# A fused decoder layer on one core: one low part of the seven-product blocks on GpSimd, drains in another order, one barrier between stages, sample taps dealt over tiles, fold turns a stage earlier

## The chip, the cores and the metric

The kernel runs on one core of one Trainium2 chip. The metric is the device time of one execution in microseconds (us), the median of three runs. Its engines are PE (TensorE, matrix products; PEld is its weight load), DVE (VectorE), ACT (ScalarE), POOL (GpSimd) and SP (SyncE, which here starts most transfers). Each has its own instruction list and runs it in order; they meet only at semaphores.

## The reference

One layer over 2048 prompt rows and 8 x 4 sample rows of width 1024, all in float32:

```python
h = rms_norm(x, norm1_g) * (1 + sc1) + sh1          # sc, sh, g from silu(c) @ w_ada + b_ada
q, k, v, u = jnp.split(h @ w_in, ...)               # 512, 512, 512, 1024 columns
q, k = rms_norm(q per head), rms_norm(k per head)
o_attn = attend(q, k, v)                            # three dilated windows, merged
glu = u[..., :512] * sigmoid(u[..., 512:])
dw = causal depthwise conv of width 31 over [history; glu], + bias
o_conv = silu(layer_norm(dw)) @ w_pw2
x = x + g1 * (concat[o_attn, o_conv] @ w_o)
h2 = rms_norm(x, norm2_g) * (1 + sc2) + sh2
x = x + g2 * (square(relu(h2 @ w_ff1)) @ w_ff2)     # 1024 -> 4096 -> 1024
```

The outputs are x for prompt and sample rows, the keys and values of the window, and the last 30 GLU rows.

## The kernel before

Every large product is made of three PE products: each operand is split into a rounded high part (ACT writes it) and a low part, the difference (DVE or POOL writes it), and PE adds high x high, high x low and low x high. The names end in `_hi` and `_lo`.

The program is a row of stages, each one `nc.Block()` with its own instruction lists for the five engines. The times are those of the profile below:

- stage 1, 0 to 65 us: conditioning vectors (`mod`), weights `vu_w`, the first two row tiles. `modulate(i)` (L498) scales tile i into `h_full`, `low_second` (L673) writes the low part of tile 1.
- stage 2 (`vu_`), 66 to 385: values and GLU for 17 row tiles (one has the 32 sample rows). `partial(q)` (L1035) and `select(q)` (L1045) are small PE steps for a quarter of the later conditioning vectors; `products(i, columns)` (L1010) are the large ones.
- stage 3 (`qk_`), 386 to 605: queries and keys for 17 tiles; tile 0 of this stage is the one with the sample rows. PE runs `products(u)`; ACT squares; DVE takes sums, inverse roots (`head_norms`) and the key's gain (`key_gain`). DVE also has the sample rows' convolution here, 31 taps, and 80 late steps of the prompt's (`late_op`, L302).
- stage 4 (`pa_`), 606 to 879: attention of the prompt. Stage 5 (`sa_`), 880 to 959: attention of the sample rows.
- stage 6 (`mx_`), 960 to 1231: layer norm, the products with `w_pw2` and `w_o`, the second norm. It begins with 16 PE turns (transposes) of `w_pw2`, which ACT copies out (L2371), and then folds `w_pw2` into `w_o`, eight groups of products (L2613).
- stage 7 (`ff_`), 1232 to 2624: the MLP, in 3 runs over rows (352, 352 and 336 columns wide per half), each of 8 blocks over the hidden width. In runs 1 and 2, blocks 1 to 6 are "seven-product" blocks: a 2 x 2 product by seven products of sums. Their operands for the second product are 14 high parts on ACT (`sum_high`) and 14 low parts on DVE (`seven_low_part`); the sums they come from are `seven_sum` on DVE. PE's results of the second product leave in 28 drains, `accumulate_seven(b, d)` (L3413), also on DVE. The last two sums (6 and 7) are `zz[0]` and `zz[3]`, the sources of low parts 12 and 13, which both belong to operand S4, the one that PE uses last. POOL writes the low parts of the weights (L3126, 128x512 each, a ring of `WR = 7` slots) in the order in which PE takes them.

Between two stages stands `end_stage()`. The Block itself closes with a barrier of all engines; then:

```python
            nc.clear_and_free_semaphores(list(stage_sems))
            stage_sems.clear()
            nc.all_engine_barrier()
```

The clear runs on POOL, so the stage boundary has two barriers and a clear between them. It is called at six places.

## Time and profile before

| | |
|---|---|
| runs | 2627.72, 2631.33, 2631.54 us; median 2631.33 us |
| profiled execution | 2625.87 us, span of the trace 2624.0 us |
| granted clock of TensorE, mean | 0.986 |
| busy | PE 2521.2 us (96%), DVE 1902.5 (73%), ACT 1282.2 (49%), POOL 1256.0 (48%) |
| instructions | 46483 |

The span runs from the first to the last instruction of the trace; the profiled execution's own time has 1.9 us more around it. The median of the runs is 5.5 us above the profiled execution. PE is busy nearly all the time, so what matters is where it still stands idle, and where it runs at the lower of its two clocks (a granted clock of 0.5 instead of 1).

### The profile page before, as it was taken

How to read it: one execution, taken by the hardware profiler on the slowest of the kernel's cores; microseconds unless marked ns; L12 is line 12 of the kernel's file. 1: busy time of each engine (PE TensorE's matmuls, PEld its weight loads, DVE VectorE, ACT ScalarE, POOL GpSimd, SP SyncE). 2: the span in 40 equal slices, each digit the busy share in tenths (PEclk: the TensorE clock that was granted, in tenths of full speed). 3: DMA queues.
4: the chain of work that ended last, by engine and by line, in shares of the span. 5: the costliest groups of instructions: out<-in, count | busy, mean ns of one | idle time of the engine just before them, and what ended most of it. 6: DMA issues, size and time to landing. Idle time of an engine off the chain costs nothing.

```text
span 2624.0 us, 46483 instructions
## 1 busy us (share of the span) xinstructions
PE 2521.2 (96%) x16058; PEld 2234.5 (85%) x16058; DVE 1902.5 (73%) x4173; ACT 1282.2 (49%) x3188; POOL 1256.0 (48%) x846
## 2 busy tenths in 40 slices
PE   6999989998999889998999999999999999999998
PEld 3788857886777647887999999999999999999998
DVE  4268889997999657876866666566777776667776
ACT  4443313448898534655444333435554453555443
POOL 0000000007999015664655555546676674767673
PEclk9999999998999999999999999999999999999999
DMA  7867625843445884664457766565555566555443
GB/s 298 287 214 238 207 95 188 288 139 119 142 142 164 303 331 149 190 219 128 144 198 256 252 231 226 192 200 167 181 182 181 178 192 214 184 173 158 133 133 125
DMA packets 362198, 507.85 MB, mean 194 GB/s; under 512 B 29338, under 2 KB 277894, under 8 KB 352102
## 3 DMA queue, kind: packets, MB, share of 16 engines
q1 hardware_dynamic: 340090, 455.45, 52.8%
q0 software_dynamic: 4272, 39.19, 4.2%
q10 hardware_dynamic: 17604, 10.24, 1.3%
q8 instruction: 131, 2.15, 0.3%
q14 instruction: 101, 0.83, 0.1%
HBM read 405.10 MB, written 171.81 MB: 220 GB/s over the span
## 4 chain that ended last, share of the span: by engine, by line
PE 22%; POOL 17%; issue 12%; DVE 2%; ACT 0%; POOLq 0%; DMA 0%; SPq 0%; DVEq 0%; ACTq 0%
POOL ff_w_lo L3126 14%; PE ff_u_ps L3646 5%; PE ff_u_ps L3648 5%; PE ff_u_ps L3647 5%; POOL over_acc L3126 2%; PE opening_ps L3646 2%; PE opening_ps L3648 2%; PE opening_ps L3647 2%; PE ff_out_ps L3641 0%; DVE ff_h_hi L3335 0%; DVE ff_h_lo L3338 0%; DVE ff_e L3328 0%; DVE ff_e L3330 0%; POOLq L2793 0%; DVE ff_e L3325 0%
## 5 line engine op out<-in xcount | busy, mean ns | idle before, releaser
L3126 POOL TENSOR_TENSOR ff_w_lo<-gluT,ff_w_hi 128x512 fp32r<-128x512 f32 x450 | 629.1, 1408 | 383.3 <-ACT ff_w_hi L3175 381.2
L3175 ACT ACTIVATE ff_w_hi<-gluT 128x512 fp32r<-128x512 f32 x450 | 278.5, 625 | 295.2 <-PE ff_u_ps L3648 184.2
L3646 PE MATMUL ff_u_ps<-ff_a_hi,ff_w_hi 128*128 128x352 f32 (+1 forms) x696 | 225.1, 323 | 17.6 <-DVE ff_a_lo L3403 14.3
L3648 PE MATMUL ff_u_ps<-ff_a_hi,ff_w_lo 128*128 128x352 f32 (+1 forms) x696 | 223.6, 321 | 0.0
L3647 PE MATMUL ff_u_ps<-ff_a_lo,ff_w_hi 128*128 128x352 f32 (+1 forms) x696 | 223.2, 321 | 0.0
L1780 ACT ACTIVATE pa_score<-pa_score,pa_stat 128x256 f32<-128x256 f32 (+1 forms) x384 | 172.4, 452 | 31.6 <-DVE pa_stat L1722 29.2
L3646 PE MATMUL ff_u_ps<-ff_h_hi,ff_w_hi 128*128 128x352 f32 (+1 forms) x548 | 176.0, 321 | 0.5 <-POOL ff_w_lo L3126 0.5
L3648 PE MATMUL ff_u_ps<-ff_h_hi,ff_w_lo 128*128 128x352 f32 (+1 forms) x548 | 175.4, 320 | 0.0
L3647 PE MATMUL ff_u_ps<-ff_h_lo,ff_w_hi 128*128 128x352 f32 (+1 forms) x548 | 175.0, 319 | 0.0
L302 DVE SCALAR_TENSOR_TENSOR vu_dwp<-gluT,tapT,vu_dwp 128x512 f32<-128x512 f32 x240 | 161.1, 748 | 0.8 <-DVE rstd L210 0.8
L1021 PE MATMUL vu_z_ps<-vu_w_hi,last_hi 128*128 128x512 f32 (+1 forms) x384 | 152.1, 396 | 2.5 <-DVEq L959 2.5
L1022 PE MATMUL vu_z_ps<-vu_w_lo,last_hi 128*128 128x512 f32 (+1 forms) x384 | 150.3, 391 | 0.0
L1023 PE MATMUL vu_z_ps<-vu_w_hi,last_lo 128*128 128x512 f32 (+1 forms) x384 | 150.1, 391 | 0.0
L3646 PEld LDWEIGHTS ff_u_ps<-ff_a_hi,ff_w_hi 128*128 128x128 f32 x696 | 131.6, 189 | 20.7 <-DVE ff_a_lo L3403 16.5
L3647 PEld LDWEIGHTS ff_u_ps<-ff_a_lo,ff_w_hi 128*128 128x128 f32 x696 | 131.9, 189 | 0.0
L3648 PEld LDWEIGHTS ff_u_ps<-ff_a_hi,ff_w_lo 128*128 128x128 f32 x696 | 131.4, 189 | 0.0
L3646 PE MATMUL opening_ps<-ff_a_hi,ff_w_hi 128*128 128x352 f32 (+1 forms) x368 | 119.3, 324 | 8.0 <-DVE ff_a_lo L3403 7.1
L3126 POOL TENSOR_TENSOR over_acc<-gluT,over_dwq 128x512 fp32r<-128x512 f32 x75 | 104.8, 1397 | 40.4 <-ACT over_dwq L3175 40.0
L3648 PE MATMUL opening_ps<-ff_a_hi,ff_w_lo 128*128 128x352 f32 (+1 forms) x368 | 118.6, 322 | 0.0
L3647 PE MATMUL opening_ps<-ff_a_lo,ff_w_hi 128*128 128x352 f32 (+1 forms) x368 | 118.4, 322 | 0.0
L1620 POOL TENSOR_SCALAR pa_tap_x<-gluT,tapT 128x1024 f32<-128x1024 f32 x40 | 113.9, 2847 | 3.0
L2584 PE MATMUL mx_z_ps<-mx_wo_hi,mx_m_hi 128*128 128x512 f32 (+1 forms) x272 | 110.6, 406 | 0.0
(559 smaller groups left out, 7718.7 us busy)
## 6 DMA issues: line engine op xcount, KB each, us to landing
gluT<-in_w_ff_dram SPq DMA_DIRECT2D x196, 256.0 KB, 3.4
gluT<-in_w_ff_dram SPq DMA_DIRECT2D x64, 512.0 KB, 5.3
gluT<-tu_d SPq DMA_DIRECT2D x112, 256.0 KB, 3.0
gluT<-td_d SPq DMA_DIRECT2D x96, 256.0 KB, 3.2
out_new_k_sample_dram<-in_cache_k_dram SPq DMA_DIRECT2D x40, 511.0 KB, 5.2
out_new_v_sample_dram<-in_cache_v_dram SPq DMA_DIRECT2D x40, 511.0 KB, 5.4
dwq<-in_w_ada_dram SPq DMA_DIRECT2D x32, 512.0 KB, 8.6
gluT<-in_cache_k_dram SPq DMA_DIRECT2D x16, 1024.0 KB, 8.8
```

What stands on the lines that cost most here:

```text
L302: return v.scalar_tensor_tensor(out=out, in0=x, scalar=tap(j, c), in1=out, op0=ALU.mult, op1=ALU.add)
L1021: pe.matmul(z, hi, w_hi[:, k, cols], start=k == 0, stop=False)
L1022: pe.matmul(z, hi, w_lo[:, k, cols], start=False, stop=False)
L1023: mm = pe.matmul(z, lo, w_hi[:, k, cols], start=False, stop=k == KT - 1)
L1620: step(pool.tensor_scalar(tap_x[:], gluT[:, c, j + SEQ - LATE:j + SEQ], tap(j, c), None, ALU.mult))
L1780: act.activation(prob[:, u % 4, hh, cols], score[:, u % 4, hh, cols], ACT.Exp, bias=stat[:, p, t, 0, h:h + 1], scale=-1.0, accum_out=stat[ ...
L2584: pe.matmul(z_ps[c][0:n], hi, wo_hi[:, k, cols], start=k == 0, stop=False)
L3126: pool.tensor_tensor(slot_view(w_lo, s), src, slot_view(w_hi, s).bitcast(F32), ALU.subtract).then_inc(w_lod, 1)
L3175: act.activation(slot_view(w_hi, s), src, ACT.Copy).then_inc(w_hid, 1)
L3646: pe.matmul(out, w_hi[s % WR][:, w], hi, start=first, stop=False, skip_group_check=more)
L3647: pe.matmul(out, w_hi[s % WR][:, w], lo, start=False, stop=False, skip_group_check=more)
L3648: return pe.matmul(out, w_lo[s % WR][:, w], hi, start=False, stop=last, skip_group_check=more)
```

## The change

Seven places are edited.

1. `end_stage` only collects the semaphores; a new `clear_ended` clears them on POOL just before the next Block. The second barrier is gone. The next stage uses other semaphores.
2. Stage 1: tile 1 is modulated half by ACT and half by DVE, and split in halves, as tile 0 was.
3. Stage 2: PE's `products(1, (1,))` goes ahead of `partial(0)`, and `select(0)` goes behind `products(1, (2,))`. SP no longer waits at the end of the stage for the store of the window's GLU rows; ACT waits for it in stage 3.
4. Stage 3: PE takes both column halves of tile 0 for each row k of the weights, as their low parts arrive. DVE's 31 sample taps, which stood ahead of the first `head_norms`, are dealt over tiles 1 to 12, two or three to a tile. ACT's load of the Exp table is issued ahead of the last tile's scaling; the last query store no longer waits for the keys.
5. Stage 5 now holds the PE turns of `w_pw2` with their copies, and the turn of the first convolution tile. They write to PSUM buffers that both stages share. On SP the loads of `w_pw2` and `w_o` go ahead of six loads of `mx_stat`.
6. Stage 7, seven-product blocks, DVE: sum 7 goes one drain earlier, low part 12 goes from behind drain 20 to behind drain 17.
7. The same blocks: low part 13 leaves DVE for POOL (`last_low`), ahead of a weight's low part.

The diff, cut to its core:

```diff
 
     whole = ExitStack()
     with whole:
-        stage_sems = []
+        stage_sems, ended_sems = [], []
 
         def sem(name):
             stage_sems.append(nc.alloc_semaphore(name=name))
@@ -126,9 +126,14 @@
 
         def end_stage():
 
-            nc.clear_and_free_semaphores(list(stage_sems))
+            ended_sems.extend(stage_sems)
             stage_sems.clear()
-            nc.all_engine_barrier()
+
+        def clear_ended():
+
+            if ended_sems:
+                nc.clear_and_free_semaphores(list(ended_sems))
+                ended_sems.clear()
 
         def keep(name, shape, dt=F32):
...
@@ -704,7 +704,9 @@
                                 if k == 3:
                                     v.wait_ge(late_in, 32)
                                 table(k)
-                        low_second()
+                        modulate_half(1)
+                        low_half(1, 0)
+                        low_half(1, 1)
 
             end_stage()
...
@@ -1066,12 +1068,12 @@
                         pe.sem_inc(z_pe, NC)
                         products(1, (0,))
                         turn_hist(0)
+                        products(1, (1,))
                         partial(0)
-                        products(1, (1,))
                         turn_hist(1)
-                        select(0)
                         turn_x(2)
                         products(1, (2,))
+                        select(0)
                         partial(1)
                         pe.wait_ge(hist_cp, 2)
                         turn_glu(0)
...
@@ -1360,7 +1372,9 @@
                         v.wait_ge(gain_in, 16 * 3)
                         v.tensor_scalar(qgain[:], qgain[:], -float(DH) ** -0.5, None, ALU.mult).then_inc(gain_set, 1)
                         view = lambda t: t[:].rearrange("p c (b t) -> p c b t", t=DS)
-                        for j in range(TAPS):
+
+                        def sample_tap(j):
+
                             w = tapT[:, j * CC:(j + 1) * CC].unsqueeze(2).unsqueeze(3).to_broadcast([P, CC, DB, DS])
                             if j == 0:
                                 step(v.tensor_tensor(view(dwS), gluS[:, :, :, j:j + DS], w, ALU.mult))
@@ -1368,7 +1382,9 @@
                             else:
                                 step(v.tensor_tensor(view(dwT), gluS[:, :, :, j:j + DS], w, ALU.mult))
                                 step(v.tensor_tensor(dwS[:], dwS[:], dwT[:], ALU.add))
-                        v.sem_inc(dw_done, 1)
+                            if j == TAPS - 1:
+                                v.sem_inc(dw_done, 1)
+
                         for u in range(NT + 1):
                             if u < NT:
                                 head_norms(u)
...
@@ -1379,6 +1395,8 @@
                             for o in range(QK_OPS * u // (NT - 1), QK_OPS * min(u + 1, NT - 1) // (NT - 1)):
                                 late_op(v, cstep, o)
                             key_gain(u)
+                            for j in range(TAPS * max(u - 1, 0) // (NT - 4), min(TAPS * u // (NT - 4), TAPS) if u else 0):
+                                sample_tap(j)
                         cstep.need(cstep.last)
 
                     @block.tensor
...
+
+                        def first_products():
+
+                            n = rows_of(tile_at[0])
+                            for k in range(KT):
+                                pe.wait_ge(w_lod, k + 1)
+                                hi, lo = h_hi[0][:, k, 0:n], h_lo[0][:, k, 0:n]
+                                for c in range(2):
+                                    z, cols = z_ps[c][0:n, :], slice(c * 512, (c + 1) * 512)
+                                    pe.matmul(z, hi, w_hi[:, k, cols], start=k == 0, stop=False)
+                                    pe.matmul(z, hi, w_lo[:, k, cols], start=False, stop=False)
+                                    mm = pe.matmul(z, lo, w_hi[:, k, cols], start=False, stop=k == KT - 1)
+                                    if k == KT - 1:
+                                        mm.then_inc(z_pe, 1)
 
                         def turn_qk(u):
                             n = rows_of(tile_at[u])
...
@@ -1897,6 +1935,9 @@
                     sp.wait_ge(o_done, 1)
                     store_sample(sp, 0)
                     sp.dma_start(mx_dwt[:, 0], dw_d[:, :, 0:P]).then_inc(dw_in[0], 16)
+                    sp.wait_ge(k_pe, 8 * DB)
+                    sp.dma_start(wp_raw, I["w_pw2"][0].rearrange("(k p) c -> p k c", p=P)).then_inc(wp_in, 16)
+                    sp.dma_start(wl_raw, I["w_o"][0, AW:D, :].rearrange("(k p) c -> p k c", p=P)).then_inc(wl_in, 16)
                     sp.wait_ge(pa_st_out, 16 * 3)
                     rows = mx_stat[:].rearrange("p a i s h -> p a i (s h)")
                     sp.dma_start(rows[:, 0], st_d[0]).then_inc(stat_in, 16)
@@ -1904,9 +1945,6 @@
                     for m in range(4):
                         sp.dma_start(rows[:, 1, m:NT:4], by_row[m].rearrange("p (n c) -> p n c", n=NT // 4)).then_inc(stat_in, 16)
                     sp.dma_start(rows[:, 2], st_d[2].rearrange("i r c -> (i r) c").rearrange("(a p) c -> p a c", p=P)).then_inc(stat_in, 16)
-                    sp.wait_ge(k_pe, 8 * DB)
-                    sp.dma_start(wp_raw, I["w_pw2"][0].rearrange("(k p) c -> p k c", p=P)).then_inc(wp_in, 16)
-                    sp.dma_start(wl_raw, I["w_o"][0, AW:D, :].rearrange("(k p) c -> p k c", p=P)).then_inc(wl_in, 16)
                     sp.dma_start(mx_dwt[:, 1], dw_d[:, :, P:2 * P]).then_inc(dw_in[1], 16)
 
...
@@ -2001,6 +2039,17 @@
                             for c in range(4):
                                 turn(AHEAD, c)
                         values(g)
+                    pe.wait_ge(wp_in, 16)
+                    for j in range(CC):
+                        if j == 3:
+                            pe.wait_ge(wt_d, 1)
+                        for k in range(CC):
+                            mm = pe.transpose(fold_ps[j % 3][:, k * P:(k + 1) * P], wp_raw[:, k, j * P:(j + 1) * P], ident[:])
+                        mm.then_inc(wt_pe, 1)
+                        if j == 2:
+                            pe.wait_ge(dw_in[0], 16)
+                            for c in range(CC):
+                                pe.transpose(opening_ps[1][:, c * P:(c + 1) * P], mx_dwt[:, 0, c], ident[:])
 
                 @block.vector
...
@@ -2595,16 +2641,8 @@
                             mm = pe.transpose(h_ps[:, k, 0:n], x1n[0:n, k * P:(k + 1) * P], ident[0:n, 0:n])
                         mm.then_inc(S["h_pe"], 1)
 
-                    turn_dw(0)
-                    pe.wait_ge(wp_in, 16)
-                    for j in range(CC):
-                        if j == 3:
-                            pe.wait_ge(S["wt_d"], 1)
-                        for k in range(CC):
-                            mm = pe.transpose(fold_ps[j % 3][:, k * P:(k + 1) * P], wp_raw[:, k, j * P:(j + 1) * P], ident[:])
-                        mm.then_inc(S["wt_pe"], 1)
+                    pe.sem_inc(S["dw_pe"], 1)
                     pe.wait_ge(wl_in, 16)
-                    pe.wait_ge(S["wt_d"], CC)
                     for g in range(NF):
...
@@ -3141,6 +3181,13 @@
                         pool.wait_ge(sq_d, e + 1)
                         pool.tensor_tensor(a_lo[:, f, tok], z[e % 4][:, 0:w], a_hi[:, f, tok].bitcast(F32), ALU.subtract).then_inc(alo_d, 1)
 
+                    def last_low(b):
+
+                        w = RUNS[b // BLKS][1]
+                        pool.wait_ge(ahi_d, LOW0[b] + 14)
+                        pool.tensor_tensor(operand(a_lo, s_lo, "S4", 1, w), seven_source("S4", 1)[:, 0:w],
+                                           operand(a_hi, s_hi, "S4", 1, w).bitcast(F32), ALU.subtract).then_inc(alo_d, 1)
+
                     pool.sem_inc(w_lod, 1)
                     pool.sem_inc(ahl_p, 4)
...
@@ -3162,6 +3209,8 @@
                         for k in range(DOWN_SLOTS[b]):
                             if blk == BLKS - 1 and run < NR - 1 and k in (1, 3):
                                 h_low(run + 1, k)
+                            if SEVEN[b] and k == 8:
+                                last_low(b)
                             low(SLOT0[b] + up_slots(b) + k + WR)
 
...
@@ -3582,16 +3631,11 @@
                             accumulate_seven(b, 14)
                             seven_sum(b, 6)
                             accumulate_seven(b, 15)
+                            seven_sum(b, 7)
                             accumulate_seven(b, 16)
-                            seven_sum(b, 7)
                             accumulate_seven(b, 17)
-                            accumulate_seven(b, 18)
-                            accumulate_seven(b, 19)
-                            accumulate_seven(b, 20)
                             seven_low_part(b, 12)
-                            accumulate_seven(b, 21)
-                            seven_low_part(b, 13)
-                            for d in range(22, 28):
+                            for d in range(18, 28):
                                 accumulate_seven(b, d)
                             continue
                         for d in range(DN):

```

What DVE does around the sums and low parts of S4, in the first seven-product block. `ff_zz0` and `ff_zz3` are sums 6 and 7 and the sources of low parts 12 and 13; `ff_y` and `ff_e` rows are drains. Before:

```order
L3397 TENSOR_TENSOR ff_zz0_17111<-ff_zz0_17111,gluT 128x352
L3430 TENSOR_TENSOR ff_y<-opening_ps1,ff_y 128x352
L3430 TENSOR_TENSOR ff_y<-ff_u_ps2,ff_y 128x352
L3397 TENSOR_TENSOR ff_zz3_17114<-ff_zz3_17114,ff_z3_13377 128x352
L3430 TENSOR_TENSOR ff_y<-ff_u_ps3,ff_y 128x352
L3430 TENSOR_TENSOR ff_y<-ff_u_ps4,ff_y 128x352
L3430 TENSOR_TENSOR ff_y<-ff_u_ps5,ff_y 128x352
L3428 COPY ff_e167<-opening_ps0 128x352
L3403 TENSOR_TENSOR ff_a_lo<-ff_zz0_17111,ff_a_hi 128x352
L3428 COPY ff_e167<-opening_ps1 128x352
L3403 TENSOR_TENSOR ff_a_lo<-ff_zz3_17114,ff_a_hi 128x352
```

The same place on DVE in the changed kernel:

```order
L3446 TENSOR_TENSOR ff_zz0_17049<-ff_zz0_17049,gluT 128x352
L3479 TENSOR_TENSOR ff_y<-opening_ps1,ff_y 128x352
L3446 TENSOR_TENSOR ff_zz3_17052<-ff_zz3_17052,ff_z3_13357 128x352
L3479 TENSOR_TENSOR ff_y<-ff_u_ps2,ff_y 128x352
L3479 TENSOR_TENSOR ff_y<-ff_u_ps3,ff_y 128x352
L3452 TENSOR_TENSOR ff_a_lo<-ff_zz0_17049,ff_a_hi 128x352
L3479 TENSOR_TENSOR ff_y<-ff_u_ps4,ff_y 128x352
L3479 TENSOR_TENSOR ff_y<-ff_u_ps5,ff_y 128x352
L3477 COPY ff_e167<-opening_ps0 128x352
L3477 COPY ff_e167<-opening_ps1 128x352
```

The second sum moved up by one drain, the first low part by three, and the second low part is gone from this engine. It stands on POOL now, among the weights' low parts of the same block:

```order
L3166 TENSOR_TENSOR ff_w_lo3<-gluT,ff_w_hi3 128x512
L3166 TENSOR_TENSOR ff_w_lo4<-gluT,ff_w_hi4 128x512
L3188 TENSOR_TENSOR ff_a_lo<-ff_zz3_17052,ff_a_hi 128x352
L3166 TENSOR_TENSOR ff_w_lo5<-gluT,ff_w_hi5 128x512
L3166 TENSOR_TENSOR ff_w_lo6<-gluT,ff_w_hi6 128x512
```

Before, the same four weight rows followed one another there with nothing between them.

The third place is SP at the end of stage 5, behind the stores of the sample rows' attention. `gluT` is the buffer that holds `w_pw2` and `w_o`. Before:

```order
L1899 DMA mx_dwt<-dw_d 128x4x128
L1902 DMA mx_stat<-st_d 128x256
L1905 DMA mx_stat<-st_d 128x4x16 x4
L1906 DMA mx_stat<-st_d 128x16x16
L1908 DMA gluT<-in_w_pw2_dram 128x4x512
L1909 DMA gluT<-in_w_o_dram 128x4x1024
L1910 DMA mx_dwt<-dw_d 128x4x128
```

In the changed kernel:

```order
L1937 DMA mx_dwt<-dw_d 128x4x128
L1939 DMA gluT<-in_w_pw2_dram 128x4x512
L1940 DMA gluT<-in_w_o_dram 128x4x1024
L1943 DMA mx_stat<-st_d 128x256
L1946 DMA mx_stat<-st_d 128x4x16 x4
L1947 DMA mx_stat<-st_d 128x16x16
L1948 DMA mx_dwt<-dw_d 128x4x128
```

The two weight loads moved past the six loads of `mx_stat`.

## Rows read from the trace of the kernel before

**Rows 1.** The page's first part: busy time of each engine.
```profile
PE 2521.2 (96%) x16058; PEld 2234.5 (85%) x16058; DVE 1902.5 (73%) x4173; ACT 1282.2 (49%) x3188; POOL 1256.0 (48%) x846
```

**Rows 2.** What PE waited for: us in total, times, longest us.
```profile
PE ff_u_ps L3646 <- DVE ff_a_lo L3403: 14.3, 8, 1.9
...
PE qk_z_ps L1399 <- DVE qk_w_lo L1359: 8.3, 3, 5.8
PE opening_ps L3646 <- DVE ff_a_lo L3403: 7.1, 4, 1.9
...
PE vu_q_ps L1042 <- DMA dwq<-in_w_ada_dram: 2.5, 2, 1.6
```

**Rows 3.** PE in a seven-product block of run 1: start, duration, instruction, [idle].
```profile
1933.61 0.43 PE L3646 MATMUL opening_ps<-ff_a_hi,ff_w_hi 128*128 128x352 f32 x1 [1.66 <-DVE ff_a_lo L3403]
1933.88 0.32 PE L3647 MATMUL opening_ps<-ff_a_lo,ff_w_hi 128*128 128x352 f32 x1
```

**Rows 4.** DVE at the same place.
```profile
1928.72 0.51 DVE L3397 TENSOR_TENSOR ff_zz<-ff_zz,ff_z 128x352 f32<-128x352 f32 x1
...
1930.88 1.17 DVE L3403 TENSOR_TENSOR ff_a_lo<-ff_zz,ff_a_hi 128x352 fp32r<-128x352 f32 x1
...
1932.41 1.15 DVE L3403 TENSOR_TENSOR ff_a_lo<-ff_zz,ff_a_hi 128x352 fp32r<-128x352 f32 x1
```

**Rows 5.** ACT and POOL at the same place.
```profile
1929.27 0.50 ACT L3227 ACTIVATE ff_a_hi<-ff_zz 128x352 fp32r<-128x352 f32 x1 [0.28 <-DVE ff_zz L3397]
...
1929.07 2.59 POOL L3126 TENSOR_TENSOR ff_w_lo<-gluT,ff_w_hi 128x512 fp32r<-128x512 f32 x2 [2.39 <-ACT ff_w_hi L3175]
...
1936.54 1.29 POOL L3126 TENSOR_TENSOR ff_w_lo<-gluT,ff_w_hi 128x512 fp32r<-128x512 f32 x1 [1.84 <-ACT ff_w_hi L3175]
```

**Rows 6.** PE at the same wait in three consecutive blocks of run 2.
```profile
2332.26 0.64 PE L3646 MATMUL opening_ps<-ff_a_hi,ff_w_hi 128*128 128x336 f32 x1 [1.93 <-DVE ff_a_lo L3403]
...
2387.68 0.42 PE L3646 MATMUL ff_u_ps<-ff_a_hi,ff_w_hi 128*128 128x336 f32 x1 [1.92 <-DVE ff_a_lo L3403]
...
2441.53 0.65 PE L3646 MATMUL ff_u_ps<-ff_a_hi,ff_w_hi 128*128 128x336 f32 x1 [1.90 <-DVE ff_a_lo L3403]
```

**Rows 7.** POOL's low parts of activations: ns min/median/max, first and last start.
```profile
L3142 POOL TENSOR_TENSOR ff_a_lo<-gluT,ff_a_hi x18: 900/1048/1247, 1250.5 to 2200.3; 128x352 fp32r<-128x352 f32 x12, 128x336 fp32r<-128x336 f32 x6
```

**Rows 8.** `end_stage`'s first and last step, six times: ns, first and last start us.
```profile
L129 POOLq DRAIN  x6: 89/101/129, 65.1 to 1231.2; - x6
...
L131 SPq EVENT_SEMAPHORE  x6: 17/17/17, 65.8 to 1231.9; - x6
```

**Rows 9.** The end of stage 1, in order of time.
```profile
59.65 2.90 ACT L505 ACTIVATE c_all<-mod_both,modT,gain 128x128 f32<-128x128 f32 x8 [3.54 <-PE mod_both L592]
...
63.67 1.22 DVE L675 TENSOR_TENSOR last_lo<-c_all,last_hi 128x1024 fp32r<-128x1024 f32 x1 [2.62 <-ACT last_hi L516]
```

**Rows 10.** SP's wait for the store of the window's GLU rows, end of stage 2.
```profile
SPq L812 <- DMA out_new_conv_sample_dram<-vu_glu: 2.2, 1, 2.2
```

**Rows 11.** DVE lines of stage 3: ns min/median/max, first and last start; a tap's share.
```profile
L1359 DVE TENSOR_TENSOR qk_w_lo<-dwq,qk_w_hi x8: 1220/1225/1226, 387.0 to 398.5; 128x1024 fp32r<-128x1024 f32 x8
...
L1320 DVE TENSOR_REDUCE qk_ssq<-qk_sqr x16: 1199/1214/1220, 420.1 to 585.8; 128x16 f32<-128x1024 f32 x15, 32x16 f32<-32x1024 f32 x1
...
L1369 DVE TENSOR_TENSOR qk_dwT<-gluS,tapT 128x128 f32<-128x128 f32 x30 | 8.8, 294 | 1.0
```

**Rows 12.** Busy time of each engine in the bulk of stage 3, with instruction counts.
```profile
420.00:600.00 180.00, 175.22 (x838) 145.50 (x836) 166.51 (x334) 91.21 (x358) 1.00 (x2) 1.00 0.65 216
```

**Rows 13.** The end of stage 3, ACT.
```profile
602.01 1.28 ACT L1310 ACT_TABLE_LOAD   x1
```

**Rows 14.** SP before the end of stage 5, and PE at the start of stage 6.
```profile
943.21 8.01 SPq L1905 DMA_DIRECT2D mx_stat<-st_d  x4
...
959.61 0.63 PE L2549 MATMUL opening_ps<-ident,mx_dwt 128*128 128x128 f32 x4 [2.80 <-PEq L131]
...
964.81 1.55 PE L2613 MATMUL opening_ps<-gluT 128*128 128x512 f32 x3 [1.19 <-DMA gluT<-in_w_o_dram]
```

99 lines of the change are left out of this document (56 added, 43 removed).

## The prediction

> **What bounds the kernel now.** I read the page's first part first: PE is busy 2521 of 2624 us and no other engine above 1902 [rows 1]. So a change gains only where PE stands idle, or where it runs at its lower clock, and the list of what PE waited for is the next view. Its largest line, in two parts because two PSUM buffers alternate, is the wait of L3646 for a low part from DVE, 21.4 us in 12 waits [rows 2]: one for each seven-product block (6 in run 1, 6 in run 2). It is the only wait in the MLP that repeats. The other lines that the change touches are the wait for the weights' low parts at the start of stage 3 (8.3) and for a conditioning weight in stage 2 (2.5) [rows 2]. What no wait line shows as one sum are the six stage ends, where every engine stands still.
>
> **Seven-product blocks.** PE begins S4 at 1933.61 after 1.66 idle [rows 3]; without the wait it would have begun 1.66 + 0.16 earlier (the interval of two matmuls, where the record of the one before ends 0.16 after the next could start), at 1931.79. Its first matmul then takes 0.43 instead of 0.32 [rows 3], and the next starts 0.27 later instead of 0.16. A block so loses 1.66 + 0.16 + 0.11, about 1.9, in run 1. In run 2 the idle is 1.90 to 1.93 [rows 6], so about 2.15. I take 1.85 and 2.15: 6 x 1.85 + 6 x 2.15 = **24.0 us** if the wait goes wholly.
>
> Does it go? DVE is behind there: it works without a gap, and low part 13 runs 1932.41 to 1933.56, low part 12 1930.88 to 1932.05 [rows 4]. After the change, sum 7 moves ahead of one drain of about 0.43 and so ends near 1928.8 instead of 1929.23 [rows 4]. ACT's rounding of it, 0.50 long, began at 1929.27 right behind the sum [rows 5]; it can begin near 1929.0, since a weight's rounding stands ahead of it, and ends at 1929.5. POOL has nothing to do before 1929.07, for it waits 2.39 for ACT [rows 5], and low part 13 stands ahead of that next weight part. Its price on POOL is not in these blocks of the trace; the nearest rows are POOL's own low parts of the same shape, 0.90 to 1.25, middle 1.05 [rows 7]. I take 1.2, since DVE works on its low part at the same time: 1929.5 to 1930.7. On DVE, low part 12 comes after drain 17, three drains (1.3) earlier: 1929.6 to 1930.8. Both lie 1.0 before PE needs them at 1931.79. So the whole 24.0 is mine, with 1.0 to spare. Lower bound: if low part 13 took 2.5 on POOL and the others slid too, half of the wait would stay.
>
> What POOL does is now later. Its two weight parts start after 1930.7 instead of 1929.07, and it runs up to about 3 us behind with the wait of PE gone. It was idle again ahead of 1936.54, for 1.84 [rows 5], and it has the ring of seven slots, 1.9 us of PE each, ahead. It catches up within the ring. DVE's drains now come one low part (1.15) and one order earlier, so PSUM banks come free earlier. Cost 0.
>
> The GPSIMD Engine Reference page of the Trainium skill (Key points) says that GpSimd shares its SBUF interfaces with VectorE, with contention for DVE instructions that have two SBUF inputs; that speaks against putting the two low parts side by side. In the trace DVE's two low parts take 1.15 and 1.17 with POOL at work on a weight beside them [rows 4, 5], so the rule, where it bites, is already in that duration. If both low parts were stretched by half again, S4 would be ready near 1931.4, still in time, and the sum would not change.
>
> **The clock.** Two of the six waits of run 2 are followed by a first matmul of 0.64 and 0.65 instead of 0.42 [rows 6]: a stretch at the lower of the two clock levels, 1.2 GHz. From 2332.26 to 2387.68, behind such a start, a block takes 55.42; from 2387.68 to 2441.53, behind a start of 0.42, it takes 53.85 [rows 6]. So a slow start costs 1.5. Two of them: **3.0 us**, if the clock stays up when PE doesn't stand idle.
>
> **Six stage ends.** From the drain on POOL to the release of SP the second barrier and the clear take 0.7, at the first (65.1 to 65.8) and at the last (1231.2 to 1231.9) [rows 8]. The clear stays, on POOL alone, beside the next stage's first work. 6 x 0.65 = **3.9 us**.
>
> **Stage 1.** The last chain is 8 ACT steps of 2.90, ACT's rounding, DVE's low part of 1.22 that ends at 64.89 [rows 9]. With four steps on each engine (ACT 1.45), halves of the rounding and of the low part, both engines overlapped, I have the end at 63.8, where PE also ends: **1.1**.
>
> **Stage 2.** PE waits 2.5 for conditioning weights in `partial(0)` [rows 2]. With 24 matmuls of 0.23 (5.5 us) ahead of it, they are there: +2.5. `select` now stands right ahead of `partial(1)`, and the copy between them costs some 0.7 of it. **1.8**. SP's wait at the end of the stage, 2.2 for a store [rows 10], goes; DVE and the other stores end 1.5 to 2 after PE anyway, so I take 0.5 of it.
>
> **Stage 3, a loss.** DVE is as full as PE here: 166.5 and 175.2 busy of 180 [rows 12], and DVE's short instructions leave about 0.04 between one and the next, so it is in truth never idle. `head_norms` begins at 420.1 and again, 15 tiles later, at 585.8 [rows 11]: 11.05 each, the first about 8.4. Before it, from 399.7 (the last low part is 1.22 long from 398.5 [rows 11]), lie the 31 taps, 61 instructions of 0.294 and 0.03 between [rows 11], about 20 us. PE has tiles 0 to 2 ready by then. With the taps dealt, DVE wants tile 0's sums at 399.7, and PE and ACT give them near 402.5: 2.8 idle. Tile 0 takes 8.4, to 410.9; tile 1 is complete near 413.3 (48 matmuls behind tile 0, and its squares; a matmul of 512 columns at 0.23, an estimate from the 0.16 of 352 columns): 2.4 idle. Then two to three taps (1.3 to 1.9) make a tile 13.2 against PE's 12.0 (180 us by 838 matmuls, 56 a tile [rows 12]), so DVE is the later one from there, and it does the same work as before with 5.2 idle put in. The two idles stand at the end of the stage: **-5.1**. PE's own earlier start on tile 0 (some 3 of the 8.3 [rows 2]) isn't cashed, since DVE ends the stage.
> The end of the stage: the table load of 1.28 stood between two of ACT's last copies [rows 13]; it moves to where ACT waits for DVE. With the small activation and the order of stores: **+1.1**.
>
> **Stage 5 to 6.** PE starts at 959.61 and its first fold product at 964.81 [rows 14]: 5.2 of turns and a wait for `w_o`. The turns go ahead of the barrier, behind the last attention products (some 4 us of PE, for which DVE's last steps of 1.8 give cover). The loads go up past `mx_stat`'s, of which the four of L1905 alone hold SP for 8.0 from 943.21 [rows 14], so `w_o` lands some 15 us earlier. The six loads themselves then end later, and the last engine at the barrier is SP or ACT's copy. I take the stage end 2 later and the folds 3.4 earlier after the barrier (PE's 2.80 idle at the start [rows 14] stays). DVE's layer norm loses 1.4 to nobody's wait. **+1.4** beside the 0.65 counted; bounds -3 (SP's loads end late) and +3.
>
> **Sum.** 24.0 + 3.0 + 3.9 + 1.1 + 1.8 + 0.5 - 5.1 + 1.1 + 1.4 = 31.7. The profiled execution took 2625.9, so 2594.2; the median of the runs is 5.5 above it, so **2599.6**. A measurement of this kernel tells about 0.2% (5.3 us) from no change.
>
> **Rivals.**
> - *Stage 3 loses nothing.* PE, not DVE, ends it, so that the idles of DVE are slack and PE's earlier start counts for 3. For it: PE is the busier of the two [rows 12]. Against: DVE's row starts are even to the end. 5 to 8 less: about 2593. Chance 0.15.
> - *Stage 5 grows.* SP's six loads, each behind 3 to 8 us of a full queue [rows 14], end after the turns, and stage 6's norm starts late. 5 more: about 2605. Chance 0.13.
> - *The S4 wait stays in part.* ACT's rounding of sum 7 comes as late as now (1929.27) and POOL takes 2 or more; then S4 is ready at 1932 to 1933, and half of the 27 stays: 2599.6 + 13 = about 2612. Chance 0.10.
> - *Slower.* `last_low` holds POOL's list until ACT has rounded sum 7. Should POOL reach it much earlier than ACT is ready and the weights' low parts behind it come late, PE would wait for them in each of 12 blocks. To eat 31.7 it needs 2.6 a block beyond the ring's cover, that is POOL ending its backlog some 8 us later than I have it; it gives 2637 at 3.1 a block. POOL's idle times of 2.39 and 1.84 speak against it [rows 5]. Chance 0.02.
> - *The wait only moves*: DVE is late elsewhere in the block, at a drain that frees a PSUM bank, and the 27 us stay: near 2627. Chance 0.02.
>
> The forecast itself has 0.58. Its own range is 2595 to 2604; the rivals beside it widen this to 2591 to 2611, which leaves out about 2 in 10. Faster by over 0.2%: 0.58 + 0.15 + 0.13 + 0.10 = 0.96; same 0.02; slower 0.02.
>
> **What would show each step.** The line "PE L3646 <- DVE a_lo" is gone from PE's waits or has turned into one of under 0.3 for POOL; seven-product blocks stand 53.85 apart in both parities of run 2, and under 54 in run 1. All six stage ends have one barrier. `head_norms` starts near 402.5 in stage 3 on this clock, with two DVE idles of 2 to 3, and the stage is 3 to 5 longer. The first fold product comes within 3 us of stage 6's start. I am wrong if S4 is ready later than PE by more than 0.3, if the lower clock comes elsewhere in the MLP, or if DVE's idle in stage 3 isn't given back at its end.

## The result

The changed kernel took 2605.66 us (median of four runs, 2604.75 to 2608.82), the kernel before 2629.52 (2627.44 to 2631.54) beside it: a ratio of 0.9908, 95% interval 0.9894 to 0.9922. That is 23.9 us less, where 31.7 were forecast, 6.1 us above the forecast of 2599.6: outside the prediction's own range of 2595 to 2604, inside the wider one of 2591 to 2611 that takes in the rivals. The profiled execution took 2605.45 us with a span of 2603.3, against 2625.87 and 2624.0 before: 20.4 to 20.7 less. The 3.4 between 20.4 and 23.9 comes from the profiled execution of before, which lay 3.65 below its own median, where that of the changed kernel lay 0.2 below.

The part that was to carry the gain did. From the list of PE's waits in the changed kernel (us in total, times, longest):

```profile
PE qk_t_ps L1447 <- DVE qk_nrm L1367: 7.5, 4, 5.1
...
PE opening_ps L1973 <- DMA gluT<-in_cache_k_dram: 5.9, 1, 5.9
...
PE vu_xt_ps L1009 <- ACT vu_x_nrm L851: 5.1, 1, 5.1
...
PE opening_ps L2651 <- PEq L1899: 3.4, 1, 3.4
```

The 21.4 us of [rows 2] for DVE's low part have no line here at all. But four waits stand at the top that before did not have or had shorter. The seven-product block that answers to [rows 3 to 5], PE first, then DVE, POOL (start, duration, instruction, [idle]):

```profile
1933.37 0.32 PE L3692 MATMUL ff_u_ps<-ff_s_hi,ff_w_lo 128*128 128x352 f32 x1
1933.53 0.32 PE L3690 MATMUL opening_ps<-ff_a_hi,ff_w_hi 128*128 128x352 f32 x1
1933.69 0.32 PE L3691 MATMUL opening_ps<-ff_a_lo,ff_w_hi 128*128 128x352 f32 x1
```
```profile
1931.30 1.20 DVE L3452 TENSOR_TENSOR ff_a_lo<-ff_zz,ff_a_hi 128x352 fp32r<-128x352 f32 x1
```
```profile
1931.16 0.95 POOL L3188 TENSOR_TENSOR ff_a_lo<-ff_zz,ff_a_hi 128x352 fp32r<-128x352 f32 x1 [2.76 <-ACT ff_a_hi L3276]
1932.08 2.84 POOL L3166 TENSOR_TENSOR ff_w_lo<-gluT,ff_w_hi 128x512 fp32r<-128x512 f32 x2
```

PE goes from one operand to the next at its usual 0.16. POOL's low part is done at 1932.1 and DVE's at 1932.5, 1.0 ahead of the matmul at 1933.53: the margin that the prediction had. POOL's took 0.95 where I took 1.2. They don't really run side by side: DVE's began 0.14 behind POOL's and ended 0.38 behind its end. That is the rule in this trace. Of the changed kernel's low parts on DVE (L3452, 128x352 and 128x336), the 36 that began with POOL idle took 0.49 to 0.53 us. Of the 120 that began with POOL at work, 118 ended 0.36 to 0.39 us behind the end of POOL's instruction, however long that made them; the other two began in its last 0.04 and ended that far behind the next one. The same block shows all of it (DVE, then POOL):

```profile
1922.40 0.51 DVE L3452 TENSOR_TENSOR ff_s_lo<-gluT,ff_s_hi 128x352 fp32r<-128x352 f32 x1
1923.27 1.18 DVE L3452 TENSOR_TENSOR ff_s_lo<-gluT,ff_s_hi 128x352 fp32r<-128x352 f32 x1
```
```profile
1922.74 1.33 POOL L3166 TENSOR_TENSOR ff_w_lo<-gluT,ff_w_hi 128x512 fp32r<-128x512 f32 x1 [2.38 <-ACT ff_w_hi L3224]
```

Where did the rest go? I cut each execution at the first PE row of a stage. Each stretch holds the stage and the boundary behind it:

| stretch | before | changed | difference | forecast |
|---|---|---|---|---|
| to stage 2's first product | 66.23 | 64.63 | -1.6 | -1.75 |
| stage 2 | 322.09 | 326.26 | +4.2 | -2.95 |
| stage 3 | 217.80 | 220.82 | +3.0 | +3.35 |
| stage 4 | 274.36 | 272.92 | -1.4 | -0.65 |
| stages 5 and 6 | 354.18 | 354.41 | +0.2 | -2.7 |
| MLP, to its last turn | 1381.56 | 1356.92 | -24.6 | -27 |

Stages 1, 3 and 4 are within 0.8 of the forecast. Stage 2 is 7 us worse than forecast, stages 5 and 6 are 3 worse, the MLP 2.4. One execution of each kernel stands behind the table; a second one of before's code in stages 1 to 6 (the first experiment) had 67.6 and 323.7 in the first two stretches, and was within 0.5 in the others. Stage 2 is the question. Its wait of 5.06 is a new one; the rows around it, of the changed kernel (ACT, SP, POOL):

```profile
102.83 1.06 ACT L834 ACTIVATE vu_x_nrm<-vu_x_in 128x1024 f32<-128x1024 f32 x1 [12.52 <-DMA vu_x_in<-in_x_prompt_dram]
```
```profile
86.57 0.30 SPq L786 DMA_DIRECT2D mod_d<-vu_g_rows  x1
86.91 0.36 SPq L757 DMA_DIRECT2D vu_x_in<-in_x_prompt_dram  x1
```
```profile
85.86 0.52 POOL L174 DMA_DIRECT2D out_new_k_sample_dram<-in_cache_k_dram  x1 [25.61 <-PE vu_z_ps L1025]
```

ACT stands 12.5 us for a row tile that SP asked for at 86.91, right behind its store of `select(0)`'s rows at 86.57. A microsecond ahead of it POOL had asked for a 4 MB copy of cached keys. The list of transfers in that stretch (issues, KB each, us to landing), first of the changed kernel, then of before:

```profile
out_new_k_sample_dram<-in_cache_k_dram POOLq DMA_DIRECT2D x1, 4088.0 KB, 16.0
...
vu_x_in<-in_x_prompt_dram SPq DMA_DIRECT2D x1, 512.0 KB, 15.8
```
```profile
out_new_k_sample_dram<-in_cache_k_dram POOLq DMA_DIRECT2D x1, 4088.0 KB, 18.1
...
vu_x_in<-in_x_prompt_dram SPq DMA_DIRECT2D x1, 512.0 KB, 4.3
```

Before, the load was issued at 90.32 and the copy at 90.98, and the load landed in 4.3. The two issues have changed places, a microsecond apart, and the load lands 11.5 us later; whether the one causes the other is tested below. TensorE's granted clock over the 30 us from 86 was 0.92 in the changed kernel and 1.00 before.

### The profile page after: what moved, and what is told of

Same layout as the page of the kernel before. It is cut to its first block and busy times, and to the rows that moved or that the text cites. A ratio compares the mean times of both kernels' runs of the same rounds, so it can differ in the third digit from the quotient of the medians.

```text
span 2603.3 us, 46434 instructions
## 1 busy us (share of the span) xinstructions
PE 2517.2 (97%) x16058; PEld 2232.5 (86%) x16058; DVE 1893.4 (73%) x4166; ACT 1281.3 (49%) x3185; POOL 1262.4 (48%) x858
```

## The experiments

Each ran beside the kernel before, on the same chip. The chips differ from one series to the next; before's median was 2629.2 to 2630.4 in all of them. Where a text calls a run "the changed kernel", its median is 2605.66 and comes from a series of its own. The runs of one kernel lie up to 6 us apart, so a difference of two medians under some 3 us says little by itself.

**The seven-product edits alone.** The kernel before with parts 6 and 7 of the change, nothing else:

```diff
+                            if SEVEN[b] and k == 8:
+                                last_low(b)
...
                             accumulate_seven(b, 15)
+                            seven_sum(b, 7)
                             accumulate_seven(b, 16)
-                            seven_sum(b, 7)
                             accumulate_seven(b, 17)
-                            accumulate_seven(b, 18)
-                            accumulate_seven(b, 19)
-                            accumulate_seven(b, 20)
                             seven_low_part(b, 12)
-                            accumulate_seven(b, 21)
-                            seven_low_part(b, 13)
-                            for d in range(22, 28):
+                            for d in range(18, 28):
```

> The kernel before with the edits of the seven-product blocks alone (parts 6 and 7 of the change). Theory: these edits carry the whole gain in the MLP. In the changed kernel the stretch from the first to the last seven-product block was 25.8 us shorter (10.8 in run 1, 15.0 in run 2), so here too: span 2624.0 - 26 = 2598, median 26 below the kernel before, which is 2 below the whole change. Rival: part of the MLP's gain comes from the other edits, which moved the stage's start against its transfers; then the gain here is under 20.

2600.44 us; ratio 0.9888 (0.9873 to 0.9903), 29.9 less than before. The MLP stretch was 1357.4, as in the changed kernel. So these edits carry the whole gain, and the other five parts together made the kernel slower: by 5.2 in the medians, by 2.0 in the spans of the profiled executions (2601.3 and 2603.3). The medians give more than the 24.1 of the MLP stretch; stage 1 alone differs by 2 to 3 us from execution to execution (see the last section), so I read sizes from the stretches.

**Order without POOL.** The changed kernel, low part 13 on DVE behind drain 18:

```diff
-                            if SEVEN[b] and k == 8:
-                                last_low(b)
...
                             seven_low_part(b, 12)
-                            for d in range(18, 28):
+                            accumulate_seven(b, 18)
+                            seven_low_part(b, 13)
+                            for d in range(19, 28):
```

> The changed kernel, but low part 13 stays on DVE, one drain behind low part 12; nothing extra on POOL. Theory: by the trace of before, DVE would have low part 12 until 1930.8, a drain of 0.43, and low part 13 until 1932.4, against PE's need at 1931.79: a wait of 0.6 and 0.3 for the slow first matmul, 0.9 in 12 blocks: 11 us slower than the changed kernel. Rival: the order alone is enough, since the order of the drains brought everything forward: within 2 us of the changed kernel, and the S4 wait does not come back.

2612.44 us; 0.9931 (0.9914 to 0.9947), 6.8 more than the changed kernel; MLP 1363.9, 7.0 more. The wait is back, shorter:

```profile
PE ff_u_ps L3690 <- DVE ff_a_lo L3450: 4.2, 8, 0.7
...
PE opening_ps L3690 <- DVE ff_a_lo L3450: 2.1, 4, 0.7
```

6.3 us in 12 waits, where I had 0.6 each. The order alone gives about 17.6 of the 24.6, and with it in place POOL gives the other 7.

**POOL without the order.** The changed kernel, with DVE's sum 7 and low part 12 in their old places:

```diff
                             accumulate_seven(b, 15)
-                            seven_sum(b, 7)
                             accumulate_seven(b, 16)
+                            seven_sum(b, 7)
                             accumulate_seven(b, 17)
+                            accumulate_seven(b, 18)
+                            accumulate_seven(b, 19)
+                            accumulate_seven(b, 20)
                             seven_low_part(b, 12)
-                            for d in range(18, 28):
+                            accumulate_seven(b, 21)
+                            for d in range(22, 28):
```

> The changed kernel with low part 13 on POOL, but DVE's sum 7 and low part 12 back in their old places (behind drains 16 and 20). Theory: low part 12 ends at 1932.05 as before, 0.26 after PE's need of 1931.79, and costs 0.26 + 0.3 a block: 6 to 7 us slower than the changed kernel, the wait line names DVE L3452 with about 0.3 each. Rival: POOL alone does it, no line in the waits and within 2 us.

2615.17 us; 0.9942 (0.9927 to 0.9957), 9.5 more; MLP 1365.8, 8.9 more. PE waits 7.6 us for L3452 in 12 waits, 0.51 each in run 1 and 0.76 in run 2, where I had 0.26. The rows of DVE and POOL say why:

```profile
1935.56 1.55 DVE L3452 TENSOR_TENSOR ff_a_lo<-ff_zz,ff_a_hi 128x352 fp32r<-128x352 f32 x1
```
```profile
1935.44 2.83 POOL L3166 TENSOR_TENSOR ff_w_lo<-gluT,ff_w_hi 128x512 fp32r<-128x512 f32 x2
```

Low part 12 took 1.55 here, in all six blocks of run 1, instead of 1.17 [rows 4]. It began 0.12 behind the start of POOL's first weight part and ended 0.38 behind its end (1936.73). In the kernel before it began 0.51 into one, and so had less of it to stand out: the low part's length is what is left of POOL's instruction, and 0.38. Neither half of the change is enough; each leaves 6 to 8 us of waits. POOL alone gives 15.7 of the 24.6, and with it in place the order the other 8.9.

**`select(0)` back in its place.** The changed kernel, one line moved:

```diff
                         turn_hist(1)
+                        select(0)
                         turn_x(2)
                         products(1, (2,))
-                        select(0)
                         partial(1)
```

> The changed kernel with select(0) of stage 2 back in its place ahead of turn_x(2); products(1, (1,)) stays ahead of partial(0). Theory: in the changed kernel SP stood at the store of select(0)'s result until 86.57 and so issued the load of the next row tile at 86.91, behind POOL's 4 MB-class cache copy of 85.86; the load landed near 102.8 and PE waited 5.06 at 112.86. With select(0) early, SP issues that load ahead of the copy: PE's wait at 112.86 is gone, ACT's wait for the load falls from 12.5 to under 1, at a price of about 0.4 for PE's wait on ACT's copy before select(0): 4 to 5 us less than the changed kernel. Rival: the copy simply comes earlier against the loads, whatever SP does: the wait stays at 4 to 5 us, and the time is that of the changed kernel.

2597.63 us; 0.9876 (0.9862 to 0.9891), 8.0 less than the changed kernel. Stage 2 took 318.1 instead of 326.3. SP and POOL:

```profile
83.03 0.63 SPq L786 DMA_DIRECT2D mod_d<-vu_g_rows  x1
88.47 0.36 SPq L757 DMA_DIRECT2D vu_x_in<-in_x_prompt_dram  x1
```
```profile
89.17 0.53 POOL L174 DMA_DIRECT2D out_new_k_sample_dram<-in_cache_k_dram  x1 [27.52 <-PE vu_z_ps L1025]
```

The load is ahead of the copy again, and PE's wait is gone. The gain is 3 above what I expected, since the clock too stays at 1.00 over the 30 us from 86, and a wait of 0.51 at 86.60 goes.

**The copy later.** `select(0)` stays where the change put it; POOL's first cache copy waits for one more row tile:

```diff
                         for i in (2, 5, 8):
-                            pool.wait_ge(z_pe, NC * i)
+                            pool.wait_ge(z_pe, NC * max(i, 3))
```

> The changed kernel, select(0) where the change put it, but GpSimd's first copy of cached keys in stage 2 waits for one row tile of products more (three instead of two, some 11 us later). Theory: the 5 us wait at 112.86 comes from that copy, issued at 85.86, standing in front of the load of the next row tile, issued at 86.91; with the copy behind the load the wait is gone and TensorE's clock stays up: 7 to 8 us less than the changed kernel, stage 2 at 318 to 319 us as in e4_select_back. Rival: select(0)'s place delays something else (DVE's second mod rows waited 9.2 us for SP's store), the load is late by its own queue: the wait stays above 3 and the time is within 2 us of the changed kernel.

2598.87 us; 0.9886 (0.9869 to 0.9902), 6.8 less than the changed kernel; stage 2 took 318.8, and the load, issued at the same point, is there in time:

```profile
86.19 0.36 SPq L757 DMA_DIRECT2D vu_x_in<-in_x_prompt_dram  x1
```
```profile
90.49 1.06 ACT L834 ACTIVATE vu_x_nrm<-vu_x_in 128x1024 f32<-128x1024 f32 x1 [0.90 <-DMA vu_x_in<-in_x_prompt_dram]
```

So it was the copy in front of the load: with `select(0)` still late and SP still behind its store, moving the copy alone cures it. Stage 2 was 326.3 to 327.3 in all seven kernels that had both, and 318.0 to 318.8 in the four that had the one or the other cured.

**PE's whole order of stage 2 as before.**

```diff
                         turn_hist(0)
-                        products(1, (1,))
                         partial(0)
+                        products(1, (1,))
                         turn_hist(1)
+                        select(0)
                         turn_x(2)
                         products(1, (2,))
-                        select(0)
```

> The changed kernel with PE's whole order in stage 2 as before: partial(0) ahead of products(1, (1,)), select(0) ahead of turn_x(2). Beside e4_select_back it tells what the products ahead of partial(0) are worth. Theory: the 2.5 us waits of partial(0) for the conditioning weights come back, and e4's gain of 3 over the kernel before in this stage goes with them; x_in is loaded in time as in e4: 5 to 6 less than the changed kernel, 2.5 slower than e4_select_back. Rival: GpSimd's copy comes earlier by the one barrier that is gone and still passes the load: the wait of 5 stays and it is slower than the changed kernel.

2603.16 us; 0.9896 (0.9881 to 0.9910), 2.5 less than the changed kernel, 5.5 more than with `select(0)` alone put back. Stage 2: 323.5 against 318.1. The wait that the products had covered is back, and the clock falls behind it:

```profile
74.23 1.08 PE L1044 MATMUL vu_q_ps<-dwq,vu_cT 128*32 128x256 f32 x8 [3.09 <-DMA dwq<-in_w_ada_dram]
...
78.20 0.63 PE L1023 MATMUL vu_z_ps<-vu_w_hi,last_hi 128*128 128x512 f32 x1
```

A product of 512 columns takes 0.63 there instead of 0.39. The products ahead of `partial(0)` are worth 5.4, twice what I took from the wait alone. The waits of `partial(0)` come to 3.5 in this run (3.09 and 0.43) against 2.5 in the kernel before.

**Taps back in front.** The changed kernel, the 31 taps ahead of the loop as before:

```diff
+                        for j in range(TAPS):
+                            sample_tap(j)
                         for u in range(NT + 1):
...
-                            for j in range(TAPS * max(u - 1, 0) // (NT - 4), min(TAPS * u // (NT - 4), TAPS) if u else 0):
-                                sample_tap(j)
```

> The changed kernel with the 31 sample taps back ahead of the first head_norms in stage 3; PE's first_products, the early table load and the last query store stay. Theory: DVE's two idles of 2.39 and 2.42 at tiles 0 and 1 are gone, and since DVE sets the stage's end, stage 3 ends 4.8 earlier: 4 to 5 us less than the changed kernel, and PE's wait of 5.1 for DVE qk_nrm near the end is gone. Rival: PE is the bound and the dealt taps cost nothing: the same time as the changed kernel, within 1 us in stage 3.

2601.01 us; 0.9888 (0.9872 to 0.9904), 4.6 less than the changed kernel; stage 3 took 216.7 instead of 220.8. PE's wait of 5.1 for DVE near the stage's end is gone (one of 5.2 stands at its first turn, where tile 0's norms come after the taps). DVE in the changed kernel, its first two tiles:

```profile
404.44 1.21 DVE L1332 TENSOR_REDUCE qk_ssq<-qk_sqr 32x16 f32<-32x1024 f32 x1 [2.39 <-ACT qk_sqr L1285]
...
415.35 1.22 DVE L1332 TENSOR_REDUCE qk_ssq<-qk_sqr 128x16 f32<-128x1024 f32 x1 [2.42 <-ACT qk_sqr L1285]
```

Two idles of 2.4 at the start of the stage, given back by 4.1 of its end. DVE is the bound, as argued. PE's earlier products of tile 0 and the early table load, which this run keeps, show little: 216.7 stands against 217.8 and 217.4 in two executions of before's code, and one barrier of that is gone too.

**Taps in the idles.** `select(0)` back, and four taps ahead of tile 0, four behind it, 23 dealt:

```diff
+                        for j in range(4):
+                            sample_tap(j)
                         for u in range(NT + 1):
...
-                            for j in range(TAPS * max(u - 1, 0) // (NT - 4), min(TAPS * u // (NT - 4), TAPS) if u else 0):
+                            for j in range(*((4, 8) if u == 0 else (8 + (TAPS - 8) * (u - 1) // (NT - 4), 8 + (TAPS - 8) * u // (NT - 4)) if u <= NT - 4 else (0, 0))):
```

> e4_select_back, and in stage 3 four taps ahead of tile 0's head_norms, four behind tile 0, the other 23 dealt over tiles 1 to 12. Theory: the taps fill the two idles of DVE (2.4 each; four taps take 2.6) and nothing else changes: 4 to 4.5 us less than e4_select_back (2597.6), so about 2593.5. Rival: what ends the stage is the tail of ACT and PE behind the last tiles, which does not move: within 1 us of e4_select_back.

2592.23 us; 0.9855 (0.9837 to 0.9872): the fastest, 13.4 less than the changed kernel and 5.4 less than with `select(0)` alone. Stage 3 took 216.9, no better than with all taps in front. Of the two idles one of 0.98 is left at tile 0. The profiled execution is 16.0 shorter than that of the changed kernel: 8.2 in stage 2 and 4.0 in stage 3, which the two edits explain, and 3.4 in stages 5 and 6, where nothing was edited (below).

**Two barriers again.**

```diff
-            ended_sems.extend(stage_sems)
+            nc.clear_and_free_semaphores(list(stage_sems))
             stage_sems.clear()
+            nc.all_engine_barrier()
```

> The changed kernel with the clear and the second barrier of before back at the six stage ends. Theory: 0.65 to 0.7 at each: 3.9 us slower than the changed kernel, if none of it is hidden. Rival: where the next stage starts with a wait for a transfer (the cache keys at the start of stage 5, the first tiles of the MLP) the barrier is hidden, and where it moves SP's loads against GpSimd's cache copies it changes more than its own length: between -2 and +2.5 us, and the PE wait at 112.86 of stage 2 changes.

2608.57 us; 0.9912 (0.9896 to 0.9928), 2.9 more than the changed kernel, with overlapping intervals. The stretches are longer by 1.3 (stage 1), 1.0, 1.3, 0.8 and 1.1 (stages 5 and 6, two boundaries), and 0.8 shorter for the MLP, which has no boundary behind it: 4.7 in all, for 3.9 expected. The barriers' own share is seen where PE stands ahead of the first product of a stage: 0.73, 0.60, 0.37, 0.57, 0.16 and 0.36 longer than in the changed kernel, from stage 2 to the MLP, 2.8 in all. So the barriers are on the path, but at the later boundaries part of each is hidden behind another wait: 2.8 for 3.9.

**Part 5 undone.** Turns of `w_pw2`, their copies and the loads' order back in stage 6 and behind `mx_stat`, as the diff in the section on the change has them with the signs exchanged.

> The changed kernel with part 5 undone: the PE turns of w_pw2, their copies and the turn of the first convolution tile are back in stage 6, and SP's loads of w_pw2 and w_o are back behind the mx_stat loads. Theory: part 5 bought nothing, because SP's mx_stat loads, moved behind the weights, hold the barrier and TensorE's clock falls behind that wait. Stages 5 and 6 together were 354.2 us in the kernel before and 354.4 in the changed one although two barriers of 0.65 are gone; so undone, they are 353 to 354: the time is that of the changed kernel, 0 to 1.5 less. Rival: part 5 is worth the 1.4 us of the prediction and something else in these stages took it (the landing of the cache keys): then undone it is 1 to 2 slower.

2606.90 us; 0.9914 (0.9899 to 0.9929), 1.2 more than the changed kernel; stages 5 and 6 took 353.4 instead of 354.4, 1.0 less. The two disagree in sign, and neither is clear of noise. Where in stage 5 the time lies tells more. Early in it PE waits for the first cached keys, whose loads part 5 doesn't touch. The wait, and a later place where nothing but DVE is waited for, in the kernel before, in the changed one and in this run:

```profile
891.80 3.63 PE L1935 MATMUL sa_k_ps<-ident,gluT 128*128 128x128 f32 x16 [2.48 <-DMA gluT<-in_cache_k_dram]
...
923.92 1.28 PE L1935 MATMUL sa_k_ps<-ident,gluT 128*128 128x128 f32 x10 [0.82 <-DVE sa_kTt L2014]
```
```profile
897.71 1.97 PE L1973 MATMUL opening_ps<-ident,gluT 128*128 128x128 f32 x8 [5.90 <-DMA gluT<-in_cache_k_dram]
...
930.68 1.06 PE L1973 MATMUL opening_ps<-ident,gluT 128*128 128x128 f32 x8 [0.82 <-DVE sa_kTt L2063]
```
```profile
897.33 1.97 PE L1972 MATMUL opening_ps<-ident,gluT 128*128 128x128 f32 x8 [4.80 <-DMA gluT<-in_cache_k_dram]
...
929.18 1.06 PE L1972 MATMUL opening_ps<-ident,gluT 128*128 128x128 f32 x8 [0.82 <-DVE sa_kTt L2051]
```

| | before | changed | part 5 undone |
|---|---|---|---|
| stage 5's first product to the later place | 43.4 | 46.1 | 43.8 |
| from there to the MLP's first product | 310.7 | 308.4 | 309.6 |

The first row has the wait for the keys, the second all that part 5 edits. The second row was 307.1 to 309.7, 308.45 in the mean, in the eight kernels with part 5 as in the changed one and one barrier at each boundary. So part 5 gives some 1.1, near the 1.4 forecast, by one execution without it. What took it away is the keys, 2.6 later than before. That is the rival of the text above. The keys' wait was 2.3 and 2.5 in two executions of before's code and 2.96 to 6.14 in the others, this one included; what makes them late no run shows.

SP does hold the barrier into stage 6, as the theory said; the changed kernel's SP and PE:

```profile
955.00 8.39 SPq L1946 DMA_DIRECT2D mx_stat<-st_d  x4
963.44 2.21 SPq L1947 DMA_DIRECT2D mx_stat<-st_d  x1
965.69 1.07 SPq L1948 DMA_DIRECT2D mx_dwt<-dw_d  x1
```
```profile
967.60 5.37 PE L2651 MATMUL opening_ps<-gluT 128*128 128x512 f32 x8 [3.38 <-PEq L1899]
```

PE's last turn ends at 964.2. SP issues until 966.76, and the barrier stands for it. PE waits 3.38, and over the 5 us behind it the granted clock was 0.66. But before had a wait of 2.80 at this boundary [rows 14] and a granted clock of 0.66 over the 5 us behind it as well, so little of this is new.

**Part of `mx_stat` ahead.** The changed kernel, three of the six `mx_stat` loads ahead of SP's wait for the key turns:

```diff
-                    sp.wait_ge(k_pe, 8 * DB)
-                    sp.dma_start(wp_raw, ...)
-                    sp.dma_start(wl_raw, ...)
...
                     for m in range(4):
+                        if m == 2:
+                            sp.wait_ge(k_pe, 8 * DB)
+                            sp.dma_start(wp_raw, ...)
+                            sp.dma_start(wl_raw, ...)
```

> The changed kernel with another order of SP at the end of stage 5: three of the six mx_stat loads ahead of SP's wait for PE's key turns, then w_pw2 and w_o, then the rest. Theory: in the changed kernel the barrier into stage 6 stands for SP, whose last load issues at 966.8 while PE and DVE are done at 964.2; SP stood idle from 942.0 to 945.8 for the key turns. With that gap filled SP is done up to 3.7 earlier, so the first fold starts 2 to 2.5 us earlier and TensorE's clock does not fall behind it (it was granted 0.66 in the 5 us behind the wait, worth 1.5 to 2): 3 to 4 us less than the changed kernel. Rival: w_pw2 and w_o land later by what the stat loads take, PE waits for them before the turns and the folds: no gain or 1 to 3 us lost.

2607.58 us; 0.9911 (0.9894 to 0.9927), 1.9 more. Neither account was right. The weights were in time for the turns, but SP was not done earlier, since each issue took longer:

```profile
962.20 5.06 SPq L1948 DMA_DIRECT2D mx_stat<-st_d  x1
967.30 3.28 SPq L1949 DMA_DIRECT2D mx_dwt<-dw_d  x1
```

PE's last turn ended at 967.6 here and SP at 970.6, 3.0 apart. By these rows an earlier start did not let SP finish earlier; that a full queue is what holds it is likely but not shown.

**`mx_stat` from GpSimd.** The fastest kernel, with the six loads on POOL behind PE's key turns:

```diff
+                    pool.wait_ge(k_pe, 8 * DB)
+                    pool.wait_ge(pa_st_out, 16 * 3)
...
-                    sp.dma_start(rows[:, 0], st_d[0]).then_inc(stat_in, 16)
+                    pool.dma_start(rows[:, 0], st_d[0]).then_inc(stat_in, 16)
```

> e7_split_taps with the six mx_stat loads issued by GpSimd, on its own queue, in stage 5 behind PE's key turns; SP issues only the two convolution tiles, w_pw2 and w_o there. Theory: SP no longer holds the barrier into stage 6; the stage ends with PE's last turn or DVE's last sum, 2.5 us earlier, and the clock does not fall: 3 to 4 less than e7_split_taps (2592.2). Rival: the transfers, not SP's issuing, are what is late (the rings are full until the stage's end), so the loads land as late on another queue and DVE waits for them in stage 6: within 1 us of e7_split_taps.

2593.25 us; 0.9856 (0.9839 to 0.9873), the same as without (2592.23). SP no longer held the barrier, but in the fastest kernel it had hardly held it: PE waited 1.49 there, against 1.09 here. And another wait came:

```profile
945.48 0.62 PE L2002 MATMUL sa_o_ps<-first_k,sa_probT 128*32 128x512 f32 x1 [2.55 <-DMA sa_vn<-in_cache_v_dram]
...
955.31 3.67 PE L2654 MATMUL opening_ps<-gluT 128*128 128x512 f32 x8 [1.09 <-PEq L1901]
```

The last cached values, which PE did not wait for at this place in the fastest kernel, are now late by 2.55. Stages 5 and 6 took 355.2 against 351.0. What was taken off SP came back as a wait for a transfer.

## Why the prediction was right, and where not

- **S4's wait**: right, in mechanism, margin (1.0) and size; 24.6 with the clock's share instead of 27. Run 1 gave 10.8 of 11.1, run 2 15.0 of 15.9. Two small new waits, of 0.79 and 0.71, stand at the end of run 2; in run 0, where nothing was edited, one wait is 0.7 longer, one of 0.8 is new and one is 0.4 shorter. The rival of a wait that only moves is out. One sign was set wrong: with a wait of 1.92 gone, blocks of run 2 could not still stand 53.85 apart. They stand 51.7 apart, and 53.8 in run 1 instead of 55.7.
- **POOL's price and backlog**: right; 0.91 to 0.96 for 1.2, no wait of PE for a weight's low part in these blocks. I took 1.2 for each of two low parts that share the time; in the trace POOL's runs undisturbed and DVE's ends 0.38 behind it. The sum is the same.
- **Stage 3**: right, the forecast's only loss: idles of 2.39 and 2.42 for 2.8 and 2.4, and 4.1 to 4.6 of the end (stretch and median) for 5.1. The +1.1 for the stage's end was not tried by itself; what is seen of it is under 1.
- **Stage 1 and barriers**: the stretch of stage 1 came out at 1.6 for 1.75, in a stretch that varies by more than that, and part 2 was not undone in any run. The barriers were worth about 2.8 of the 3.9.
- **Stage 2**: the step that failed. I wrote that `select` now stands right ahead of `partial(1)` and that "the copy between them costs some 0.7". I costed PE's own wait and overlooked that SP stands in its list behind the store of `select`'s rows, that the next row tile's load is behind SP, and that POOL's 4 MB copy would pass it. In its place stands a loss of 8.2 us against a gain of 5.4, of which I had 2.5. Both wrong sizes have the clock in them. The 0.5 for SP's wait at the stage's end was not tried by itself.
- **Stages 5 and 6**: the term of 1.4 for part 5 was about right (some 1.1). The step that failed is one that I put at nothing: PE's wait for the first cached keys, which was 5.90 instead of 2.48 and made stage 5 2.6 longer. It and the rest eat the 1.4 and the two barriers. The rival "stage 5 grows" has the number (stage 5 grew by 3.8) but not the cause: SP and the turns have 1.2 of it.
- **The level**: I put the forecast 5.5 above the profiled execution. Before's medians in five series lay 3.3 to 4.5 above it, and the changed kernel's lies 0.2 above its own. For the profiled execution the sum says 2594.2 and 2605.45 was measured, 11.3 more. So the level hid part of the miss: that the median came out only 6.1 off is luck, and so is that it lies on the 2605 of the rival "stage 5 grows".

## What to carry over

Before a small step on the bounding engine is moved later, follow its product through the queue that stores it: everything behind that store on the same queue moves too, and it may fall behind a large copy from another engine. An engine that is as full as the bounding one gives nothing back: of 4.8 us of idle put into it early, 4.1 came out at the stage's end. Try the parts of a combined change apart: here parts 6 and 7 held all of the gain, and undoing one line and filling two idles gave another 12 us. And when a stage comes out longer than forecast, set its waits beside those of the kernel before one by one, those ahead of the edit too.
